# Building the norm rows from a diagonal tile, and the places of the hooks around them, in a single-core decoder kernel

## The reference

```python
def rmsnorm(x, g):
    xf = x.astype(jnp.float32)
    y = xf * lax.rsqrt(jnp.mean(xf * xf, axis=-1, keepdims=True) + EPS)
    return (y * g.astype(jnp.float32)).astype(x.dtype)
```

## Time and profile before

| | |
|---|---|
| median of 3 runs | 2654.5 us (2652.2 to 2655.4) |
| profiled execution | 2652.2 us, its span 2650.4 us |
| TensorE busy | 2620.3 us, 99% |
| DVE busy | 1350.0 us, 51% |
| ACT busy | 966.5 us, 36% |
| POOL busy | 118.9 us, 4% |
| TensorE's mean granted clock | 0.999 |

### The profile page before, as it was taken

One profiled execution on the slowest core, in us unless ns is written; L12 is line 12 of the kernel. 1 busy time (PEld: TensorE's weight loads), 2 busy tenths in 40 slices (PEclk: granted clock), 3 DMA queues, 4 the chain that ended last, 5 costly groups with the idle time before them and its releaser, 6 DMA issues.

```text
span 2650.4 us, 31309 instructions
## 1 busy us (share of the span) xinstructions
PE 2620.3 (99%) x12624; PEld 2142.0 (81%) x12624; DVE 1350.0 (51%) x2146; ACT 966.5 (36%) x1527; POOL 118.9 (4%) x126
## 2 busy tenths in 40 slices
PE   8999999999999999999999999999999999999999
PEld 6867888888889778888876788888888688888887
DVE  5365673664434777366558544344552155544343
ACT  3265442443225644244445432223223233422221
POOL 2000000000000000000013000000120400000000
PEclk9999999999999999999999999999999999999999
DMA  4311223222231122323221133223232022223232
GB/s 148 128 64 49 96 95 104 95 99 101 96 103 65 41 96 92 105 92 101 101 80 37 64 106 101 88 96 103 97 126 88 9 98 101 96 96 101 91 99 85
DMA packets 66480, 240.52 MB, mean 91 GB/s; under 512 B 7632, under 2 KB 7760, under 8 KB 66208
## 3 DMA queue, kind: packets, MB, share of 16 engines
q1 hardware_dynamic: 63648, 229.38, 25.5%
q0 software_dynamic: 2688, 9.14, 1.1%
HBM read 236.36 MB, written 2.13 MB: 90 GB/s over the span
## 4 chain that ended last, share of the span: by engine, by line
PE 96%; DVE 2%; ACT 2%; issue 0%; DMA 0%; SPq 0%; DVEq 0%; ACTq 0%
PE ps L438 29%; PE ps L440 29%; PE ps L439 29%; PE ps L550 2%; PE ps L570 1%; PE ps L590 1%; PE ps L849 1%; PE ps L836 1%; PE ps L519 1%; PE ps L503 0%; ACT m_E_P L1703 0%; PE ps L701 0%; ACT m_B_P L1703 0%; DVE m_wsp L887 0%; PE ps L776 0%
## 5 line engine op out<-in xcount | busy, mean ns | idle before, releaser
L438 PE MATMUL ps<-m_xs,m_wsp 128*128 128x512 f32 x2232 | 873.1, 391 | 14.8 <-DVE m_wsp L887 11.6
L439 PE MATMUL ps<-m_xs,m_wsp 128*128 128x512 f32 x2232 | 869.4, 390 | 0.0
L440 PE MATMUL ps<-m_xs,m_wsp 128*128 128x512 f32 x2232 | 869.4, 390 | 0.0
L1601 ACT ACTIVATE m_wsp<-m_raw 128x1024 fp32r<-128x1024 f32 x429 | 446.7, 1053 | 779.3 <-PE ps L440 741.5
L887 DVE TENSOR_TENSOR m_wsp<-m_raw,m_wsp 128x1024 fp32r<-128x1024 f32 x429 | 519.5, 1226 | 188.5 <-ACT m_wsp L1601 188.3
L438 PEld LDWEIGHTS ps<-m_xs,m_wsp 128*128 128x128 f32 x2232 | 419.7, 188 | 103.5 <-issue 13.1
L440 PEld LDWEIGHTS ps<-m_xs,m_wsp 128*128 128x128 f32 x2232 | 419.6, 188 | 87.7
L439 PEld LDWEIGHTS ps<-m_xs,m_wsp 128*128 128x128 f32 x2232 | 419.7, 188 | 86.1
L935 DVE TENSOR_TENSOR m_x<-m_x,ps 128x512 f32<-128x512 f32 x104 | 71.0, 687 | 316.8 <-PE ps L440 316.8
L438 PE MATMUL ps<-m_wsp,m_xs 128*128 128x512 f32 x320 | 125.8, 393 | 0.0
L440 PE MATMUL ps<-m_wsp,m_xs 128*128 128x512 f32 x320 | 125.1, 391 | 0.0
(11 more groups left out here) (292 smaller groups left out, 3186.3 us busy)
## 6 DMA issues: line engine op xcount, KB each, us to landing
m_raw<-in_w SPq DMA_DIRECT2D x429, 512.0 KB, 3.3
m_A_cb<-csum POOLq DMA_DIRECT2D x16, 256.0 KB, 3.8
m_x<-in_xT SPq DMA_DIRECT2D x4, 512.0 KB, 8.2
m_B_bias<-in_biasB POOLq DMA_DIRECT2D x8, 256.0 KB, 3.2
out<-m_x SPq DMA_DIRECT2D x8, 256.0 KB, 2.0
m_O_D<-in_decay POOLq DMA_DIRECT2D x1, 1024.0 KB, 5.0
m_O_cs<-in_ropeo POOLq DMA_DIRECT2D x1, 512.0 KB, 3.4
m_E_wt<-in_gmw POOLq DMA_DIRECT2D x1, 256.0 KB, 3.0
```

The source lines that it names most:

```text
L438: e.matmul(out, lh, rh, start=first, stop=False)
L439: e.matmul(out, lh, rl, start=False, stop=False)
L440: return e.matmul(out, ll, rh, start=False, stop=final)
L1601: e.activation(wsp[n % NSP][:, 0, :], raw[n % NRAW][:, :], ACT.Copy).then_inc(*s_hi(n))
```

## The change

It has three parts.

1. `row` becomes one matmul of 512 columns, all ones times a tile `diag`. DVE makes `diag` with one elementwise product of the identity, repeated four times, with the column broadcast. It does so behind the reciprocal, after the row before has been read. For fm the product stands later, in the evacuation of ei's tile 1.
2. Hooks on TensorE get other places.
3. Some steps of DVE and ACT get other places: the eight kvn splits, the reciprocal of the key factors, and, at ev, the evacuation of the values and the scores of the second unit.

```diff
+_ROWS = ["mix0", "ffn0", "mix1", "ffn1", "m2_0", "fm", "qa", "kva", "f2_0", "m2_1", ("ret", 0), ("ret", 1), ("ret", 2),
+         ("ret", 3), "f2_1"]
+ROW_BEFORE = dict(zip(_ROWS[1:], _ROWS))
...
+        diag = sb(ctx, "diag", [128, S])
...
                     q.wait_ge(*free[b])
-                    q.wait_ge(*d_id["id"])
-                    q.wait_ge(*s_col["both" if nm == "m2_0" else nm])
-                    for tb in range(4):
-                        i = e.matmul(ps[b][:, 128 * tb:128 * tb + 128], rc(nm)[:, tb:tb + 1].broadcast_to([128, 128]),
-                                     ident[:, :], start=True, stop=True)
-                    i.then_inc(*s_row(nm))
+                    q.wait_ge(*s_diag[nm])
+                    e.matmul(ps[b][:, :], ones[:, :], diag[:, :], start=True, stop=True).then_inc(*s_row(nm))
...
-            ffn("f1", "ffn1", {15: [xstat("ffn1")], 20: [row("ffn1")]})
+            ffn("f1", "ffn1", after_outproj("ffn1"))
...
-                     45: [row("qa")], 47: [xstat("kva", 2)], 62: [row("kva")]}
+                     44: [row("qa")], 46: [xstat("kva", 2)], 62: [row("kva")]}
...
-                    {10: [pair_sums("k", 0)], 14: [pair_sums("k", 1)]})
+                    {8: [pair_sums("k", 0)], 12: [pair_sums("k", 1)], 16: [pair_sums("k", 2)]})
...
-                    {2: [pair_sums("k", 2)], 5: [pair_sums("k", 3)], 8: [columns("k")], 11: [key_scale(0)], 12: [pair_sums("q", 0), key_scale(1)],
+                    {4: [pair_sums("k", 3)], 7: [columns("k")], 11: [key_scale(0)], 12: [pair_sums("q", 0), key_scale(1)],
...
-                         hooks={4: [pair_sums("q", 3)]})
+                         hooks={4: [pair_sums("q", 3), lambda: scores(E_units[1], "main")]})
             columns("q")()
-            scores(E_units[1], "main")
...
-                    {3: [row(("ret", 2))], 14: [ostat(3)], 20: [row(("ret", 3))]})
+                    {3: [row(("ret", 2))], 10: [ostat(3)], 20: [row(("ret", 3))]})
...
-            def factors(nm):
+            def inverse(nm, rcol):

                 q.wait_ge(*s_root[nm])
-                e.reciprocal(rc(nm)[:, 0:4], rc(nm)[:, 4:8]).then_inc(*s_col(nm))
+                e.reciprocal(rcol[:, 0:4], rcol[:, 4:8]).then_inc(*s_col(nm))
+                q.wait_ge(*s_col[nm])
+
+            def diagonal(nm, rcol):
+
+                q.wait_ge(*d_id["id"])
+                if nm in ROW_BEFORE:
+                    q.wait_ge(*s_row[ROW_BEFORE[nm]])
+                e.tensor_tensor(
+                    diag[:, :].rearrange("p (b n) -> p b n", b=4),
+                    ident[:, :].rearrange("p (o n) -> p o n", o=1).broadcast_to([128, 4, 128]),
+                    rcol[:, 0:4].rearrange("p (b o) -> p b o", o=1).broadcast_to([128, 4, 128]),
+                    ALU.mult).then_inc(*s_diag(nm))
+
+            def factors(nm, rcol):
+                inverse(nm, rcol)
+                diagonal(nm, rcol)
...
+                if g[-1] == 11:
+                    for k in range(8):
+                        xlo("kvn", k, "kvn")
...
-            over(ST["bq"], bq, {11: [lambda: [xlo("kvn", k, "kvn") for k in range(7)]]})
-            xlo("kvn", 7, "kvn")
+            over(ST["bq"], bq)
...
+                        if m == 1:
+                            diagonal("fm", rc("fm"))
                         if m in (1, 2, 4):
                             add_square(*("qa", m) if m < 3 else ("kva", 1))
                         if m == 4:
-                            factors("qa")
+                            factors("qa", E_rc[0])
...
-                if m == 2:
-                    q.wait_ge(*s_root["E", "k"])
-                    e.reciprocal(E_nrm[:, 1, :], E_nrm[:, 0, :]).then_inc(*s_col(("E", "k")))
                 if 0 <= n < 4:
                     key_scaled(2 * n)
...
                 e.tensor_tensor(E_rt[m % 2][64:96, :], E_q[96:128, m, :], E_gcs[0][96:128, :], ALU.mult).then_inc(*s_step(("eqt", m)))
+                if m == 2:
+                    q.wait_ge(*s_root["E", "k"])
+                    e.reciprocal(E_nrm[:, 1, :], E_nrm[:, 0, :]).then_inc(*s_col(("E", "k")))
...
-            def E_among(i):
-                if i == 0:
-                    scored(E_units[1])
-                    values_out(ST["ev"].groups[0])
...
             scored(E_units[0])
-            over(ST["ev"], lambda g: None)
+            over(ST["ev"], rows_out(ST["ev"], E_v, E_rc[1], s_col["kva"]), {0: [lambda: scored(E_units[1])]})
...
             rows("q")
-            over(ST["ev"], nothing)
             mean_roots("q")

             e.activation(line[:, 2:3], cf[:, 0:1], ACT.Exp)
+            over(ST["ev"], rows_out(ST["ev"], E_v, lambda ci: E_rc[1], lambda ci: s_col["kva"]))
             q.wait_ge(*s_qrot[7])
...
             exps(E_units[0])
-            rows_out(ST["ev"], E_v, lambda ci: E_rc[1], lambda ci: s_col["kva"])(ST["ev"].groups[0])
             exps(E_units[1])
```

More of the change, by code:

```diff
@@ L374, in rc @@
         def rc(nm):
-            if nm in ("qa", "kva"):
-                return E_rc[nm == "kva"]
-            if nm not in NORMS:
-                return O_rc[:, nm[1], :]
             return rcs[NORMS[nm] % 2]
@@ L408, in build @@
             sem(f"s_{n}") for n in ("conv", "silu", "ahi", "aev", "soft", "exp", "pt", "ohi"))
-        s_lo, s_xlo, s_x, s_col = (sem(f"s_{n}") for n in ("lo", "xlo", "x", "col"))
+        s_lo, s_xlo, s_x, s_col, s_diag = (sem(f"s_{n}") for n in ("lo", "xlo", "x", "col", "diag"))
         s_ev, s_step, s_tap, s_gated, s_alo, s_olo, s_ones, s_acc = (
@@ L952, in evacuate @@
                             if nm != "fm":
-                                factors(nm)
+                                factors(nm, rc(nm))
                 return evacuate
@@ L1090, in vector_program @@
             lo(3)
-            factors("mix0")
+            factors("mix0", rc("mix0"))
             lo(4)
@@ L1342, in two_norms @@
                 r1, r2 = rc("fm"), rc("m2_0")
-                factors("fm")
-                q.wait_ge(*s_col["fm"])
+                inverse("fm", r1)
                 q.wait_ge(*s_stat["m2_0"])
@@ L1347, in two_norms @@
                 e.tensor_tensor(r2[:, 4:8], r2[:, 0:4], bank("stat", "m2_0")[:, 0:4], ALU.mult).then_inc(*s_col(("both", 1)))
-                factors("m2_0")
-                q.wait_ge(*s_col["m2_0"])
+                inverse("m2_0", r2)
                 e.tensor_tensor(r2[:, 0:4], r2[:, 0:4], r1[:, 0:4], ALU.mult).then_inc(*s_col("both"))
+                q.wait_ge(*s_col["both"])
+                diagonal("m2_0", r2)
             def x_final(k):
@@ L1417, in ei @@
                         if m == 6:
-                            factors("kva")
+                            factors("kva", E_rc[1])
                         for k in range(2 * (m - 6), 2 * (m - 6) + 2):
@@ L1495, in vector_program @@
             over(ST["eq"], eq)
-            values_out = rows_out(ST["ev"], E_v, E_rc[1], s_col["kva"])
-            def E_among(i):
-                if i == 0:
-                    scored(E_units[1])
-                    values_out(ST["ev"].groups[0])
             scored, loop = attention("E", E_units, dict(
-                P=E_P, st=E_st, among=E_among, out=out_split("E"), bias=lambda u, j, s: E_mask[:, S - s["n"]:S],
+                P=E_P, st=E_st, among=nothing, out=out_split("E"), bias=lambda u, j, s: E_mask[:, S - s["n"]:S],
                 biased=lambda u, j: d_emask["emask"]))
             scored(E_units[0])
-            over(ST["ev"], lambda g: None)
+            over(ST["ev"], rows_out(ST["ev"], E_v, E_rc[1], s_col["kva"]), {0: [lambda: scored(E_units[1])]})
             q.wait_ge(*s_root["E", "q"])
@@ L1539, in ofactors @@
             def ofactors(h):
-                factors(("ret", h))
+                factors(("ret", h), O_rc[:, h, :])
             for h in range(5):
@@ L1951, in eq @@
                 q.wait_ge(*(s_sums["k", 2 + m // 2] if m < 4 else s_sums["q", (m - 4) // 2]))
-                if m == 1:
-                    mean_roots("k")
                 q.wait_ge(*s_ev["eq", m])
@@ L1957, in eq @@
                     rows("k")
+                elif m == 1:
+                    mean_roots("k")
                 elif m >= 4:
```

## The result

The changed kernel takes 2670.7 us (median of 4 runs, 2668.5 to 2672.8) against 2655.0 for the one before (4 runs, 2652.2 to 2656.0): a ratio of 1.0063, 95% interval 1.0051 to 1.0075. It is slower, by 15.7 us; 2668.3 was forecast, with 2661 to 2675. The profiled execution took 2670.8 us, its span is 2668.9.

A forecast was written before the change was run, and what follows sets the result against it. The prediction took TensorE's list of work to be the time, with fixed-place waits not made up later. Its terms summed to 13.8 us, giving 2666.0 profiled and 2668.3 as a median, range 2661 to 2675.

The forecast's parts named there:

- Rows, +0.9: Fifteen row matmuls: one wide matmul costs 0.95 us against 0.89 for four narrow ones, +0.9 us in all.
- The cheap row: Rival for the row matmuls: at the pair sums' 0.49 us, 2662.8 us; at the skill's ratio 2659; chance 0.09.
- The diagonal elsewhere, 0: Diagonal products at the out-projections, heads and other rows hide on DVE beside TensorE; cost nothing, head 2 up to 0.7.
- fm +1.2, qa +1.3: At the fm and qa rows TensorE waits for the late DVE diagonal product: +1.2 and +1.3 us.
- ffn1 +0.8: At ffn1's statistics the next weight chunk's split stands behind the diagonal product and its semaphore, both unhidden: +0.8 us.
- kvn +2.2: Entering bk, TensorE stalls for the first kvn split, now behind the last bq tile on DVE: +2.2 us.
- Keys +1.2: Key pair sums, columns and the later reciprocal delay the first key_scale; +1.2 us, bounds 0.7 and 2.9.
- Start of E, +4.8 and +0.5: Start of E attention: scores wait, then weight and ev copies precede ACT's first exponentials, +4.8; low clock stretch, +0.5 us.
- Head 3, +0.9: Head 3's statistics, moved to tile 10: TensorE waits for POOL's last sum, +0.9 us.
- The rival of a lower clock in more places: Two more low clock stretches, possible at kvn, pair sum 2 and the E start: +17.2 us, 2671.7; chance 0.22.
- ACT finding room: Rival at the start of E: chunk or ev copies find room, E costs 2.7; 2666 us or less; chance 0.13.
- the absorbed stalls: Rival: the weight stream absorbs stalls everywhere, as TensorE would wait for chunks anyway; 2654.5 us; chance 0.03.

The follow-up runs named there:

- the parts: Four kernels, each with one part of the change on the kernel before: row matmul, kvn splits, start of E, other places; 2658.6, 2657.7, 2658.5, 2658.2 us.
- the four places put back: Four versions of the changed kernel, each with one step undone or reordered: out-projection splits, old rows, ACT's queue, key reciprocal; 2669.5, 2667.2, 2669.3, 2671.0 us.
- Split first: The changed kernel, with DVE splitting the next weight chunk before forming the diagonal at the three out-projections; 2669.5 us (1.0056).
- no diagonal: The changed kernel with the old rows, four 128-column matmuls and no diagonal product on DVE; 2667.2 us (1.0046).
- Row alone: The kernel before with only the wide row matmul and its diagonal product, all else as before; 2658.6 us (1.0014).
- the hooks part: The kernel before with only the new hook places in f1, ei, ek, eq and og0 and the key factors' reciprocal and root moved; 2658.2 us (1.0014).
- The E part: The kernel before with only the new start of E: unit 1's scores inside ev, weight copy and ev copies ahead of ACT's first exponentials; 2658.5 us (1.0018).
- ACT's queue put back: The changed kernel with the weight copy ahead of the root of q and the ev copies behind the first exponentials; 2669.3 us (1.0055).

## Why the prediction was right, and where it wasn't

The direction and the range were right, 13.8 forecast and 15.7 measured, and the mechanism, waits that add because TensorE has nothing else to do, is shown by the parts and by the four places put back. That the sum came so near is in part luck: the rows and ffn1 were 2 us too dear, the diagonal elsewhere and head 3 were 3.8 us too cheap. Term by term:

- *Rows, +0.9.* Wrong in sign and small: 0.04 us less each. The retention rows were the right neighbours, and their price holds within 0.1 us a row. The cheap row of the pair sums and of the Trainium skill's ratio ("TensorE: Matmul & The Clock Gate", "Back-to-back issue gap") did not come: the row takes 1.08 us from start to start, and the four narrow ones 1.12.
- *The diagonal elsewhere, 0.* This step failed. I asked whether the row waits for it, for ffn0, f2_0 and the heads, and not what is queued behind it. It costs 0.55 at ffn0 and at f2_0, and 0.4 in the retention part, where the trace has a wait of 0.23 for m_O_at. Split first shows the mechanism for the out-projections. For the retention part no diagonal shows the cause, and the trace the way: m_O_at starts 1.1 us behind the reciprocal with the diagonal between them (2100.34 and 2101.46), and 0.4 without it (2096.92 and 2097.29).
- *fm +1.2, qa +1.3.* Waits of 1.07 and 1.19.
- *ffn1 +0.8.* A wait of 1.32 for the statistics appears, and the wait for the split shrinks from 0.9 to 0.26, as both stand in one queue. Net 0.2 us: the forecast was too large, since I took the split as unhidden when the earlier statistics bring it forward. Row alone, without the earlier statistics, does have the added 0.7.
- *kvn +2.2.* 2.1, in the whole and alone.
- *Keys +1.2.* 1.5. The waits of 1.27 and 2.21 are as forecast, and the reciprocal is what sets the end. From the columns to the first key_scale it is 5.78 us here (1401.34 to 1407.12) and 5.79 in the hooks part (1397.14 to 1402.93), with waits of 0.81 and 2.41: here the half-clock stretch lies beside DVE's work and costs nothing, there it lies behind it and costs 1.6. That the low clock at the old place cost 0.3 holds: the row part has no such stretch there and is 0.3 us faster through ek and eq.
- *Start of E, +4.8 and +0.5.* 5.2, but by other shares, so the match of the number is luck. The two waits are 1.20 and 4.84 against 0.81, 1.01 and 1.20 before, so 3.0 us more of waiting. The other 2.2 go mostly with the clock, which I had put at 0.5: the trace has some 5 us at half clock behind the long wait. The E part, with 3.4 of them, loses 5.0 and waits 0.45 at a later transpose, so the shares of the two aren't separated further. The queue's pieces are worth 1.5 to 1.9.
- *Head 3, +0.9.* Right as far as it went: 0.96 in the hooks part, without a diagonal. The diagonal adds 0.7, as POOL is held up beside DVE (waits of 0.7 and 1.4), and the profiled execution has 1.6 us of half clock behind. The runs put back had no such stretch in 3 of 4 cases (it was there with ACT's queue put back), so this last piece comes and goes.

The rival of a lower clock in more places, 2671.7, is nearer the median than my forecast, but not for its reasons: it put a stretch at kvn and one at E. The one at E is in every execution with the long wait there. Right behind the kvn pause it is in two of the six profiled executions that have the pause (split first and no diagonal, at 703 us, where it costs 1.6); these two have none at 770, where the other four have one, as the kernel before can. No execution has both, so none shows a stretch more for the pause. ACT finding room was wrong, the absorbed stalls too: over some 560 us of ordinary projections, from f2_0 to the retention part, the shift stays at 12.8 us and nothing is given back.

## What to carry to other kernels

Where one engine is busy 99% of the time, an edit elsewhere is judged by two questions: who waits for it, and what stands behind it in its own queue. The second was missed here at ffn0, f2_0 and the retention, and cost 1.5 us. Before a profile is compared with another, profile the same kernel twice: 2.2 of the 18.5 us between the spans of the first two profiles are between two executions of one kernel.

## What was not expected of the hardware

- A half-clock stretch costs up to 1.6 us where TensorE is on the path and nothing beside a wait for DVE that is longer, and one and the same kernel has it at 21 and 769 us in one execution and not in another.
- POOL's and DVE's elementwise work hold each other up when both operands of DVE lie in SBUF. POOL's sum takes 1.27 us alone and 1.59 to 2.18 beside such work. In the kernel before:

```profile
2110.36 1.19 DVE L887 TENSOR_TENSOR m_wsp<-m_raw,m_wsp 128x1024 fp32r<-128x1024 f32 x1
```

```profile
2110.51 2.17 POOL L2121 TENSOR_TENSOR m_O_h<-m_O_h,m_sq 128x512 f32<-128x512 f32 x1
```

The split started first and keeps its length; the sum is 0.9 us longer, nearly the 1.04 that the two overlap. In the changed kernel the sum at 2125.80 is ahead, and DVE's split at 2126.38 takes 2.29 and ends 1.07 us behind the sum's end. So in both one works and the other is held, and they don't both slow down. Beside a DVE instruction with an operand in PSUM (m_O_at<-ps, 0.9 us of overlap) the sum keeps its 1.27. The Trainium skill ("Trainium Architecture — The Big Picture", "What this means for kernel authors") says that these two share a port pair as an exclusive lock and not as a split of bandwidth. The traces agree, by the lengths above.
